# First attention: scores two quads ahead over twelve places, and GpSimd scales the probabilities from the second row tile on

## The reference

```python
s_s = jnp.einsum('bcgrd,bgcnld->bgrcnl', qc, ks).astype(jnp.float32) * scale
s_s = jnp.where(dist_s >= 0, s_s - slopes_g[None, :, :, None, None, None] * dist_s, NEG_INF)
p_s = jax.nn.softmax(s_s, axis=(-2, -1))
o_s = jnp.einsum('bgrcnl,bgcnld->bcgrd', p_s.astype(vs.dtype), vs)
...
o = gc[..., 0:1] * o_c + gc[..., 1:2] * o_s + gc[..., 2:3] * o_w
...
m = jnp.maximum(jnp.max(s, axis=-1, keepdims=True), sg)
e = jnp.exp(s - m)
prob = e / (jnp.sum(e, axis=-1, keepdims=True) + jnp.exp(sg - m))
o = jnp.einsum('bngrqk,bnkgd->bnqgrd', prob.astype(vb.dtype), vb)
```

## Time and profile before

| | us |
|---|---|
| median of three runs | 1626.7 (1621.56 to 1628.99) |
| the profiled execution: its time | 1627.72 |
| its span, first to last instruction | 1626.4 |
| PE busy | 1509.1 (93%) |
| DVE busy | 1133.0 (70%) |
| ACT busy | 617.4 (38%) |
| POOL busy | 711.6 (44%) |
| first attention, from the first scores to the first product of `w_o` | 145.99 to 290.62 |

### The profile page before, as it was taken

One profiled execution on the slowest core, in us unless ns is written; L12 is line 12 of the kernel. 1 busy time (PEld: TensorE's weight loads), 2 busy tenths in 40 slices (PEclk: granted clock), 3 DMA queues, 4 the chain that ended last, 5 costly groups with the idle time before them and its releaser, 6 DMA issues.

```text
span 1626.4 us, 22505 instructions
## 1 busy us (share of the span) xinstructions
PE 1509.1 (93%) x8093; PEld 1291.7 (79%) x8093; DVE 1133.0 (70%) x2372; ACT 617.4 (38%) x1536; POOL 711.6 (44%) x668
## 2 busy tenths in 40 slices
PE   5998777999999999999999999999998999899997
PEld 4787445788878887887799899889986787899886
DVE  7646566467777669647867677777777588777764
ACT  3314566231212220113454554454455355344431
POOL 6756000347767748685444034303435114524430
PEclk8997799999999999999999999999998999999999
DMA  6623000424444436553321011101102321211221
GB/s 186 196 78 99 6 1 1 143 72 150 138 128 123 139 98 222 190 193 106 123 66 40 14 53 53 32 22 52 53 27 78 124 96 52 58 48 40 65 91 52
DMA packets 115887, 142.61 MB, mean 88 GB/s; under 512 B 11048, under 2 KB 75200, under 8 KB 115776
## 3 DMA queue, kind: packets, MB, share of 16 engines
q1 hardware_dynamic: 89968, 91.77, 18.5%
q10 hardware_dynamic: 25808, 49.40, 9.3%
HBM read 132.74 MB, written 8.40 MB: 87 GB/s over the span
## 4 chain that ended last, share of the span: by engine, by line
PE 66%; DVE 15%; ACT 7%; POOL 5%; issue 4%; DMA 1%; ACTq 0%; SPq 0%; DVEq 0%; POOLq 0%
PE ps L510 18%; PE ps L512 17%; PE ps L511 17%; POOL w_lo L499 3%; PE ps L1290 2%; POOL w_hi L497 2%; PE ps L1486 2%; PE ps L924 1%; PE ps L982 1%; DVE st L2911 1%; ACT p L2130 1%; DVE newton L2375 1%; PE ps L948 1%; DVE p L2579 1%; PE ps L1500 1%
## 5 line engine op out<-in xcount | busy, mean ns | idle before, releaser
L497 POOL TENSOR_SCALAR w_hi<-w_raw 128x512 fp32r<-128x512 f32 x308 | 236.6, 768 | 639.2 <-PE ps L512 481.1
L499 POOL TENSOR_TENSOR w_lo<-w_raw,w_hi 128x512 fp32r<-128x512 f32 x316 | 443.3, 1403 | 30.4 <-ACT w_hi L1676 4.7
L510 PE MATMUL ps<-w_hi,h_hi 128*128 128x384 f32 (+2 forms) x768 | 278.4, 363 | 8.2 <-POOL w_lo L499 2.9
L512 PE MATMUL ps<-w_hi,h_lo 128*128 128x384 f32 (+2 forms) x768 | 265.8, 346 | 0.0
L511 PE MATMUL ps<-w_lo,h_hi 128*128 128x384 f32 (+2 forms) x768 | 265.4, 346 | 0.0
L510 PE MATMUL ps<-h_hi,w_hi 128*128 128x512 f32 (+1 forms) x616 | 244.5, 397 | 6.4 <-DVE h_lo L2405 2.6
L512 PE MATMUL ps<-h_hi,w_lo 128*128 128x512 f32 (+1 forms) x616 | 237.1, 385 | 0.0
L511 PE MATMUL ps<-h_lo,w_hi 128*128 128x512 f32 (+1 forms) x616 | 237.0, 385 | 0.0
L2629 DVE SCALAR_TENSOR_TENSOR mod_acc<-mod_piece,csil,mod_acc 128x512 f32<-128x512 f32 x140 | 160.3, 1184 | 19.1 <-DMA mod_piece<-in_ada_w 15.1
L510 PEld LDWEIGHTS ps<-w_hi,h_hi 128*128 128x128 f32 x768 | 146.8, 191 | 20.7 <-POOL w_lo L499 4.3
L511 PEld LDWEIGHTS ps<-w_lo,h_hi 128*128 128x128 f32 x768 | 147.2, 192 | 8.6 <-issue 0.5
(11 more groups left out here) (337 smaller groups left out, 2990.3 us busy)
## 6 DMA issues: line engine op xcount, KB each, us to landing
mod_piece<-in_ada_w ACTq DMA_DIRECT2D x96, 256.0 KB, 3.2
w_raw<-in_w_gate_up SPq DMA_DIRECT2D x88, 256.0 KB, 3.2
w_raw<-in_a_w_in SPq DMA_DIRECT2D x128, 128.0 KB, 2.3
w_raw<-in_w_down SPq DMA_DIRECT2D x22, 512.0 KB, 4.4
w_raw<-in_b_w_in SPq DMA_DIRECT2D x20, 512.0 KB, 3.7
w_raw<-in_w_out SPq DMA_DIRECT2D x16, 512.0 KB, 3.8
w_raw<-in_w_in SPq DMA_DIRECT2D x8, 512.0 KB, 3.8
w_raw<-in_w_o SPq DMA_DIRECT2D x8, 512.0 KB, 3.8
```

The costliest lines, as they stand in the source:

```text
L497: pool.tensor_scalar(hi[:, e, :], raw[:, e, :], 1.0, 0.0, ALU.mult, ALU.add).then_inc(*s["pool_step"].up())
L499: m = pool.tensor_tensor(lo[:, e, :], raw[:, e, :], hi[:, e, :], ALU.subtract)
L510: pe.matmul(out, a[0], b[0], start=start, stop=False)
L512: return pe.matmul(out, a[1], b[0], start=False, stop=stop)
```

## The change

The scores, least values and exponentials in step n are now those of quad n+2, whatever its number of slots, and two quads' slots are made ahead of the first step instead of four slots. `p1` has twelve places and `pt` eight (they were eight and twelve). On DVE, step n now begins with the reciprocal for quad n+1. In row tile 0 DVE still scales: one head ahead of the least values, one behind each slot, the others behind them. From row tile 1 on (`POOL_SCALES_FROM`) DVE stops at the reciprocal, signals `b_total`, and POOL scales the quad with the same operations (`pool_quad_scale`, new), between its last split of `w_o` and the wait at `("ff", 0)`; PE's transposes then wait for POOL's signal `b_scaled_p`. Values are done one chunk at a time, as soon as one is held.

```diff
-SLOTS_P = 8
-SLOTS_T, SLOTS_T_EARLY = 12, 5
+SLOTS_P = 12
+SLOTS_T, SLOTS_T_EARLY = 8, 5
...
+def pool_quad_scale(k, pool, q):
+
+    s, f = k.sig, k.st1[:, q.n % 8, :, :]
+    pool.wait_ge(*s["b_total"].at(q.n))
+    for e in range(PER_G):
+        slot, c0 = q.place(e)
+        p = k.p1[:, slot % SLOTS_P, c0:c0 + q.w]
+        c = (q.g * PER_G + e) * 3 + 1 + q.kind
+        if q.kind == 2:
+            m = pool.tensor_scalar(p, p, f[:, 3, e:e + 1], None, ALU.mult)
+        else:
+            m = pool.tensor_scalar(p, p, f[:, 3, e:e + 1], k.gates[:, q.t, c:c + 1], ALU.mult, ALU.mult)
+    m.then_inc(*s["b_scaled_p"].up(q.n))
...
                 if tile == ("ff", 0):
+                    for quad in quads():
+                        if quad.t >= POOL_SCALES_FROM:
+                            pool_quad_scale(k, pool, quad)
...
-    total = qs[-1].slots[-1] + 1
-    return range(0, 4) if n < 0 else [i + 4 for i in qs[n].slots if i + 4 < total]
+    if n < 0:
+        return range(0, qs[1].slots[-1] + 1)
+    return qs[n + 2].slots if n + 2 < len(qs) else range(0)
...
-VALUES_AT_ONCE = 2
+POOL_SCALES_FROM = 1
+VALUES_AT_ONCE = 1
...
-        pe.wait_ge(*s["b_scaled"].at(q.n))
+        pe.wait_ge(*s["b_scaled_p" if q.t >= POOL_SCALES_FROM else "b_scaled"].at(q.n))
...
+    if q.t >= POOL_SCALES_FROM:
+        dve.reciprocal(f[:, 3, :], total).then_inc(*s["b_total"].up(q.n))
+        return
...
-    m.then_inc(*s["b_scaled"].up(q.n))
+        if e == PER_G - 1:
+            m.then_inc(*s["b_scaled"].up(q.n))
+        yield
...
     for q in qs:
+        scaled = dve_quad_scale(k, dve, qs, qs[q.n + 1]) if q.n + 1 < len(qs) else iter(())
+        next(scaled, None)
         for slot in slots_behind(qs, q.n):
             dve_slot_least(k, dve, qs, slot)
-        if q.n + 1 < len(qs):
-            dve_quad_scale(k, dve, qs, qs[q.n + 1])
+            next(scaled, None)
+        for _ in scaled:
+            pass
```

More of the change, by code:

```diff
@@ L103 @@
     "zeroed sink_neg cmp_scored cmp_least cmp_exped cmp_ready "
-    "b_scored b_least b_aux b_exped b_sunk b_scaled b_turned b_pt b_valued o_hi o_lo "
+    "b_scored b_least b_aux b_exped b_sunk b_total b_scaled b_scaled_p b_turned b_pt b_valued o_hi o_lo "
     "scored least exped normed turned pt valued gated "
@@ L2587, in dve_quads @@
         dve_slot_least(k, dve, qs, slot)
-    dve_quad_scale(k, dve, qs, qs[0])
+    for _ in dve_quad_scale(k, dve, qs, qs[0]):
+        pass
     def outputs(o):
```

## The result

Median 1613.58 us (1611.04 to 1618.48, nine runs) against 1626.7 (1621.56 to 1628.99, nine runs too, not three): a ratio of 0.9928, with an interval of 0.9913 to 0.9943. By the ratio the change gains 11.7 us (the two medians lie 13.1 apart); the forecast was 24.7. The profiled execution, the fastest of the nine, took 1611.04 us, and its span is 1609.7.

A forecast was written before the change was run, and what follows sets the result against it. A chain of waits in the first attention was taken as the bound. Pair sums of 80.3 us, 84.3 with 5%, end it at 265.6 instead of 290.7: 1627.7 - 25.1 - 1.0 = 1602 us, range 1590 to 1634.

The forecast's parts named there:

- that chain: First attention: scores, exponentials, reciprocal, DVE scaling and PE transposes wait in a circle; about 25 us PE idle in three row tiles.
- row tile 0: First row tile of the attention, still scaled by DVE: scaling starts some 2 us earlier, and only that is carried on.
- POOL's price: POOL's scaling at 2.77 ns a column: a quad costs 3.2, 4.6 and 6.0 us for 256, 384 and 512 keys.
- POOL is cheap: Rival for POOL's scaling: 1.2 ns a column, every pair bound by PE, giving 1596 us; chance 0.10.
- POOL works back to back in row 3: Sign in the attention's row 3 that the step on lookahead is right; no size given.
- One sign that was named for "wrong": Attention quads: POOL idle between quads while PE waits for it would show the forecast wrong; no size given.
- 80.3 us ... I add half of that, 5%: 84.3: Attention from row tile 1 on: larger of PE and POOL per quad pair, plus last quad and tail, then 5%.
- fewer waits should not lower it: PE's clock in the attention: falls had followed waits, so PE's work was priced at full speed.
- ACT loses nothing and gains nothing: ACT in the attention's row tiles 1 to 3: its 19, 24 and 25 us stay below the pair sums.
- ACT's copies held by the values: Sign of a wrong forecast: ACT's turned copies wait if values fall three turns behind; cost taken as nothing.
- a middle price of POOL: Rival for POOL's scaling: 1.3 to 1.6 times the one-factor row, giving 1612 to 1625 us; chance 0.18.
- a PE that keeps a low clock: Attention: PE keeping a low clock also gives 1612 to 1625 us; no separate chance.

The follow-up runs named there:

- e2: The changed kernel with DVE scaling every quad, so the lookahead without POOL: ratio 0.9963 to the kernel before.
- e3: The changed kernel with POOL scaling but the lookahead and DVE order of the kernel before: ratio 1.0119 to the kernel before.
- e4: The changed kernel with sliding quads scaled on POOL in the two-factor form, a column of ones as second factor: 1611.4 us.
- e11: The changed kernel with ten useless matmuls filling PE's wait before the 19th transposes, in row tile 1: 1612.6 us against 1613.6.
- e9: The changed kernel with the eight copies of the outputs' high part moved from ACT to DVE: 5 us under the change.
- e1: The changed kernel with values done two chunks at a time again: 6 us longer than the change.
- e10: The changed kernel with the outputs' high part copied on DVE and POOL's two-factor form for sliding quads: 1603.9 us, ratio 0.9865 to the kernel before.
- e12: e4 with the turned copy of each quad's last chunk from row tile 1 on made by DVE instead of ACT: 1609.5 us against 1611.4.
- e6: The changed kernel with 28 useless matmuls filling three PE waits of row tile 0; row tile 0 gained nothing, whole time not given.

## Why the prediction was half right

**Right: what bound the kernel, and that the lookahead breaks that chain** (e2, e3). PE's wait for scaled probabilities fell from 17.6 us (14.6 of them for the two-factor quads) to 3.4, all for sliding ones, and DVE's wait for scores stayed (20.0), as foreseen. **Nearly right: row tile 0.** Forecast 2 us; the two profiles of the change have 1.7 and 3.4 (32.95 to 31.26 and 29.59, cut as in the table). POOL began its first quad at 175.20, forecast 178.1, and ended it at 177.36; PE came to its transposes at 178.89, forecast 181.3, without waiting for POOL.

**Wrong: POOL's price, in both directions.** 2.16, 2.6 and 3.0 us a quad with two factors (3.2, 4.6, 6.0 forecast), 3.62 with one (3.2). The rival "POOL is cheap" nearly had the two-factor price, and would have given 1596, which is further off. (It also adds the tail to a sum that holds the last pair's work already; by the prediction's prices 2.8 us stand there twice.) So the price isn't what failed; with POOL mostly idle it didn't count, save for the 3.4 us at sliding quads. "POOL works back to back in row 3" did not come either: it waits 1 to 5 us ahead of each quad there. One sign that was named for "wrong" did come: at sliding quads PE waits for POOL, which had been idle until DVE's reciprocal. The Trainium skill (GPSIMD Engine Reference, section 3.1) gives 769 ns for 512 elements in the good case: the two-factor form, 3.01 us for four, agrees with it; the one-factor form, 0.92 us for 256, doesn't.

**Failed: the sum, "80.3 us ... I add half of that, 5%: 84.3".** From the first transposes behind POOL to `w_o` it took 98.5 us, 14.2 more. The forecast held 72.6 us of PE's work (its nine pair sums added up) and 11.7 of idle time (4.4 where POOL was the larger, 4.0 for the 5%, 3.3 in the last pair and its tail); measured were 83.1 and 15.4. The difference has three parts:

- *The clock, about 6.0 us.* PE's work was priced at full speed, because "fewer waits should not lower it". The clock did not fall, but waits were left, and full speed was not reached: it was 0.89, 1.00 and 0.91 in row tiles 1 to 3 of the change (0.83, 0.95 and 0.92 before). The 6.0 are 83.1 less the 77.1 of e4's profile, cut alike (177.27 to 267.98); e11 shows 2.8 of them in row tile 3, on the same program. How much of it a given run pays is partly chance.
- *PE's idle time, 3.7 us net.* "ACT loses nothing and gains nothing" was taken from its busy time, 19 to 25 us a row tile, and so ACT stands in the sum at nothing. But its order carries the copies that PE waits for, behind exponentials and outputs: 11.8 us of waits, where the trace of before had already shown 6.8. With POOL's 3.4 at sliding quads they are nearly all of the 15.4. In the window pairs, where the forecast had POOL as the larger, PE's matmuls never waited for POOL. The step looked for ACT's trouble in the values ("ACT's copies held by the values"). e9 shows that part of it is curable.
- *PE's full-speed work, 4.5 us*: 77.1 where the prices gave 72.6. The prices came from rows in which eight transposes or twelve values stood together; now four and four alternate, as the chain of the changed kernel shows in row tile 3.

```profile
252.82 0.59 PE ps L944 x4
253.40 1.01 PE ps L968 x4
```

0.59 and 1.01 us where 0.5 and 0.92 were taken. That the alternation explains all of the 4.5 is an argument: e1, which undid a part of it, saved 0.4 us of work in row tile 2 and brought later values along.

Of the 14.2 us, 2.4 were won back by the earlier start: the stage ended 11.8 us after the forecast (277.37 against 265.6), and the median lies 11.6 above it. That these two agree is partly luck: the rest of the program moved as a block only within 3.5 us (1335.8 us behind the stage in the profile before, 1332.3 now), and the profile lies 2.5 under the median. The forecast had given 1612 to 1625 to a rival, a middle price of POOL, and added "so does a PE that keeps a low clock"; the measured time lies there, not by the price, and by the clock for less than half of what was missing. Of the contention the additions of the sinks show nothing: they took 0.16 to 0.28 us.

Most of the gain forecast was there to be had: e10, with eight copies moved off ACT and POOL's form changed, takes 1603.9 us.

## What to carry to other kernels

When a lookahead takes one wait out of a loop, price the next one from program orders, not from busy time: an engine that is busy two thirds of the time and serves two loops in order (here exponentials and copies) may have no slack if each stands behind the other. Look also at the small waits that the old kernel already has there. Moving a small piece of it (eight outputs) to an engine that the change had freed gained 5 us here; moving other copies (e12) gained nothing that could be told. And price PE's work at the clock that the stage will have: where waits stay in it, full speed is not given.

## What the runs showed of the hardware

- POOL's `tensor_scalar` with one per-partition factor and no second operation took 0.92 us for 256 columns; with two factors 0.55, and 0.77 for 512. With a useless second factor, a column of ones, it took 0.56 for 256 (e4).
- PE's clock fell to 0.50, the lower of its two levels (1.2 of 2.4 GHz), behind a wait of 2.54 us at the start of the stage and stayed there for 30 us; with ten useless matmuls in that wait it was at 1.00. The Trainium skill (TensorE: Matmul & The Clock Gate, HAM oscillation — how this bites in real kernels) describes bursts of work that begin cold behind waits, each time anew. The falls behind the same waits in both profiles of the change, and their absence where the wait was filled, agree; that it is each time does not, since behind waits of 2.05 and 1.78 us e4's clock stayed at 1.00.
- A higher clock is not always worth something: in row tile 0, eight microseconds at 1.00 in place of 0.50, with DVE busy 4.4 to 4.7 of each 5 us, shortened nothing (e6).
